# First banded attention: value matmuls moved from behind a unit's second group of scores to behind its first

## The reference

```python
def window_gqa(q, k, v, sinks):      # 16 heads of 64, 4 key heads, blocks of 128 queries
    kb, vb = bands(k), bands(v)      # each block sees the key block before, its own, and the next
    scores = jnp.einsum('bnqhgd,bnkhd->bnhgqk', qb, kb) * (ATTN_HEAD_DIM ** -0.5)
    scores = jnp.where(mask[None, :, None, None], scores, NEG)
    m = jnp.maximum(jnp.max(scores, axis=-1, keepdims=True), s)      # s: a sink logit per head
    p = jnp.exp(scores - m)
    probs = p / (jnp.sum(p, axis=-1, keepdims=True) + jnp.exp(s - m))
    out = jnp.einsum('bnhgqk,bnkhd->bnqhgd', probs.astype(v.dtype), vb)
```

## Time and profile before

| | us |
|---|---|
| median of 3 runs (3205.15 to 3207.88) | 3205.52 |
| the profiled execution | 3204.85 |
| its span | 3203.1 |
| PE busy | 3083.7 (96%) |
| DVE busy | 1696.3 (53%) |
| ACT busy | 1104.4 (34%) |
| POOL busy | 89.8 (3%) |

### The profile page before, as it was taken

How to read it: one execution, slowest core, us unless ns; L and a number is a source line. 1 busy time by engine, 2 the same in 40 slices (tenths; PEclk the granted TensorE clock), 3 DMA queues, 4 the chain that set the end, 5 groups by cost and what they waited for, 6 DMA issues and landing times. The chain is left out here.

```text
span 3203.1 us, 34628 instructions
## 1 busy us (share of the span) xinstructions
PE 3083.7 (96%) x14272; PEld 2390.1 (75%) x14272; DVE 1696.3 (53%) x2173; ACT 1104.4 (34%) x1723; POOL 89.8 (3%) x70
## 2 busy tenths in 40 slices
PE   8998999999999999999999999999999999999898
PEld 7885567788888888877777788888887686665566
DVE  7747854644444433589854533333334734566575
ACT  4215632311111111387732311111111415776452
POOL 0004510000000000000000000000000000000000
PEclk9999999999999999999999999999999999999999
DMA  4420011121222211211131111111111131000213
GB/s 148 114 94 1 1 73 38 48 79 66 79 66 73 72 48 45 86 47 47 64 114 33 47 46 47 50 49 47 46 48 52 53 119 33 20 20 14 92 56 110
DMA packets 54510, 190.96 MB, mean 60 GB/s; under 512 B 6288, under 2 KB 6672, under 8 KB 54224
## 3 DMA queue, kind: packets, MB, share of 16 engines
q1 hardware_dynamic: 54352, 188.74, 18.0%
HBM read 172.73 MB, written 14.68 MB: 59 GB/s over the span
## 5 line engine op out<-in xcount | busy, mean ns | idle before, releaser
L285 PE MATMUL PS<-H,wsp 128*128 128x512 f32 x6864 | 1615.3, 395 | 42.3 <-DVE wsp L141 16.8
L285 PEld LDWEIGHTS PS<-H,wsp 128*128 128x128 f32 x6864 | 1291.9, 189 | 349.6 <-issue 40.6
L285 PE MATMUL PS<-p,wsp 128*128 128x512 f32 (+1 forms) x3840 | 896.0, 393 | 20.8 <-DVE p L141 20.8
L285 PEld LDWEIGHTS PS<-p,wsp 128*128 128x128 f32 x3840 | 711.9, 189 | 198.7 <-ACT wsp L138 21.6
L138 ACT ACTIVATE p<-p 128x1024 f32<-128x1024 f32 (+7 forms) x426 | 360.8, 871 | 862.1 <-DVE p L144 680.5
L138 ACT ACTIVATE wsp<-raw 128x1024 fp32r<-128x1024 f32 (+1 forms) x267 | 276.9, 1040 | 694.2 <-PE PS L285 486.7
L141 DVE TENSOR_TENSOR p<-p,PS 128x1024 f32<-128x1024 f32 (+2 forms) x232 | 244.4, 1054 | 498.7 <-PE PS L285 498.7
L141 DVE TENSOR_TENSOR wsp<-raw,wsp 128x1024 fp32r<-128x1024 f32 (+1 forms) x267 | 321.7, 1207 | 156.1 <-ACT wsp L138 150.5
L141 DVE TENSOR_TENSOR p<-PS,p 128x1024 f32<-128x1024 f32 (+2 forms) x116 | 131.0, 1130 | 372.2 <-PE PS L285 347.3
L141 DVE TENSOR_TENSOR p<-p 128x1024 fp32r<-128x1024 f32 (+5 forms) x239 | 239.6, 1010 | 115.2 <-ACT p L138 112.1
L285 PE MATMUL PS<-p 128*64 128x256 f32 (+9 forms) x1432 | 279.1, 457 | 8.8 <-ACT p L138 3.1
(11 more groups left out here) (70 smaller groups left out, 1058.6 us busy)
## 6 DMA issues: line engine op xcount, KB each, us to landing
raw<-in_in_dram SPq DMA_DIRECT2D x72, 512.0 KB, 3.6
raw<-in_dn_dram SPq DMA_DIRECT2D x65, 512.0 KB, 3.5
raw<-in_up_dram SPq DMA_DIRECT2D x64, 512.0 KB, 3.5
raw<-in_out_dram SPq DMA_DIRECT2D x42, 512.0 KB, 3.5
p<-in_ada_dram SPq DMA_DIRECT2D x24, 512.0 KB, 4.5
p<-in_x_dram SPq DMA_DIRECT2D x16, 512.0 KB, 7.7
raw<-in_kv_dram SPq DMA_DIRECT2D x16, 512.0 KB, 3.6
spill_dram<-p SPq DMA_DIRECT2D x16, 512.0 KB, 3.0
```

Source lines behind the costliest of these rows:

```text
L285: return pe(lambda e: e.matmul(o, l, r, start=start, stop=stop, **kw), *a)
```

## The change

```diff
@@ attention_units, the loop over iterations u and groups j
                     for _ in range(fills[u] if fill and early else int(bool(fill) and fills[u] > 1)):
                         fill.pop(0)()
-                    if j == J - 1 and u >= 2:
+                    if j == (0 if full else J - 1) and u >= 2:
                         values(u - 2)
```

## The result

| | before | after |
|---|---|---|
| median, us | 3205.34 (3201.59 to 3207.88, 4 runs) | 3226.59 (3223.38 to 3228.7, 4 runs) |
| profiled span, us | 3203.1 | 3221.6 |
| first scores of the stage, at us | 246.26 | 243.43 |
| first matmul of the next stage, at us | 430.74 | 450.68 |
| length of the stage, us | 184.48 | 207.25 |

The ratio is 1.0068 (95% interval 1.0055 to 1.008): slower by 21 us, where 3226 was forecast. Between the two profiled executions the stage grew by 22.8 us; it began 2.8 us earlier in the one of after, and the rest behind it was 1.4 us shorter. These two differences lie in code that the change does not touch. The earlier start goes back to TensorE's clock well ahead of the stage: behind a wait of PE for DVE of 2.1 us, at the same instructions in both traces, the granted clock from 92 to 96 us was 0.73 in the execution of before and 1.00 in that of after.

What follows compares the result with a forecast made beforehand. PE was taken as the bound, with DVE and short waits close behind. Middle +18.7, end +1.6, start +1.8 and tail -1.25 sum to +20.9 us, giving 3226 us, range 3218 to 3238.

Steps and rivals of the forecast that it cites:

- The loop: Middle of the stage, one second scores to the next: a chain through softmax, copy, values and turn, 6.63 us against 5.83.
- The hand-over from copy to matmul: From the start of ACT's first copy to the value matmul that waits for it: taken as 0.64 us.
- second scores of unit 1 to unit 4: Start of the stage: three intervals, 5.75 us for the first and 5.15 for two, together 16.05: +1.8 us.
- unit 4 to unit 28: Middle of the stage: 24 intervals of 6.63 us, less 0.51 for shorter first values, 158.6 us: +18.7.
- unit 28 to unit 31: End of the stage: short groups at 5.15 us, the first interval 5.66, together 15.96: +1.6 us.
- unit 31 to the last values: Tail of the stage: a gain, 6.24 us in place of 7.49: -1.25 us.
- The chain itself: In the tail, a short group's second scores through softmax and first copy to the waiting value matmuls: 3.55 us.
- the third rival: PE falls to 1.2 GHz in part of the stage: 3242 us for one unit in four, 3291 for all; chance 0.06.
- The first: Rival: values ahead of the turn hide its waits and PE runs without a gap, -10.6 us, 3195; chance 0.04.
- The second: Rival: the new wait at the values is balanced by the turns' waits and unseen slack, 3205.5 us; chance 0.03.
- The fourth: Rival: the subtraction into H delays the second scores' reduction in every second unit, +4 us, 3230; chance 0.05.
- my 0.5: Estimated slack on DVE: subtraction done 1.5 us after the values end, next reduction due at 2.06, some 0.5 us left.

Runs made afterwards that it cites:

- the last experiment: The changed kernel in iterations 4 to 31, with the order of before in iterations 2, 3, 32 and 33: 3221.7 us, ratio 1.0057.

## Why the prediction was right

**The loop.** The step "the values want the copy, and the copy stands behind the second group's exponentials" held. The sum was 6.63 us a unit, the trace has 6.59. The largest deviation of a term is the step from the values to the turn behind them, 1.45 where the earlier trace rows had 1.52; why it is shorter was not looked into. The hand-over from copy to matmul, for which I had chosen 0.64 between 0.59 and 0.75, was 0.65.

**The terms.** Computed as in the prediction, in us, against the earlier trace rows:

| part | before | forecast | measured | 
|---|---|---|---|
| second scores of unit 1 to unit 4 | 14.21 | +1.8 | 17.42: +3.2 |
| unit 4 to unit 28 | 139.94 | +18.7 | 157.76: +17.8 |
| unit 28 to unit 31 | 14.33 | +1.6 | 15.83: +1.5 |
| unit 31 to the last values | 7.49 | -1.25 | 7.73: +0.2 |
| sum | | +20.9 | +22.8 |

These rows of the kernel after give the four bounds and the last values:

```profile
249.34 1.22 PE L285 MATMUL PS<-p 64*128 64x256 f32 x4
```
```profile
266.76 0.92 PE L285 MATMUL PS<-p 64*128 64x384 f32 x4
```
```profile
424.52 0.70 PE L285 MATMUL PS<-p 64*128 64x256 f32 x4
```
```profile
440.35 0.70 PE L285 MATMUL PS<-p 64*128 64x256 f32 x4
...
444.15 1.97 PE L285 MATMUL PS<-p 128*64 128x256 f32 x8 [2.42 <-ACT p L138]
...
448.08 1.08 PE L285 MATMUL PS<-p 128*64 128x256 f32 x8 [0.47 <-ACT p L138]
```

**Where it was off.** The tail. I expected a gain, because a turn and H left the path there. The chain itself was 0.25 us longer than forecast (444.15 - 440.35 = 3.80, forecast 3.55). PE had only one turn to do meanwhile and waited 2.42 us; behind that wait the granted clock fell (the values took 1.97 us instead of 1.08), and values to last values took 3.93 us, where 2.69 was forecast. That is the fall of the third rival at this one place, worth 1.2 us. It need not come with the wait: the last experiment's tail had a wait of 2.51 us without it.

In the start the values came in time (253.50 - 249.34 = 4.16, forecast 4.15), but they and the turn behind them ran at the lower clock, until about 256.2, which made the first interval 1.1 us longer than forecast. The last experiment shows that this happens with the old order too. The sum had PE at full speed in the terms of the start and of the tail.

The stage grew by 22.8 us in the trace, 1.9 more than forecast, and the code outside it took 4.3 us less than in the execution of before. The medians differ by 21.3, with an interval of 18 to 26 us. So that the time came within 1 us of the forecast is luck; the 18 us in the middle are not.

**The rivals.** The first (values in front of the turn hide its waits) came true in its first half: the turns' waits are gone. In the trace of the kernel before they were 6.5 us for ACT's copies and 5.0 for DVE's in the whole stage, while the new wait is 41.3, so what they gave back is far less than what the new wait costs. The second (no change) is excluded. The third (the clock falls) is excluded for the middle, where the clock was 1.00. The fourth (DVE late) was close: behind the subtraction into H the reduction still waited 0.28 us for PE, so DVE had 0.28 us to spare and not my 0.5.

```profile
352.35 0.69 DVE L141 TENSOR_TENSOR H<-PS,H 128x512 fp32r<-128x512 f32 x1 [0.96 <-ACT H L138]
...
353.33 0.96 DVE L501 TENSOR_REDUCE sm<-PS 128x2 f32<-128x768 f32 x1 [0.28 <-PE PS L285]
```

## What to carry to other kernels

Moving an instruction group earlier in a queue moves cover as well as work: ask for which chain it was the cover, and add that chain up from the instruction behind which the gap opens to the one that closes it. If that sum is larger than the work left in between, the difference is paid in every iteration. Where an engine finishes a long softmax ahead of a short copy that another engine waits for, the place of the copy in its queue decides (15 us of 21 here). And a subtraction that waits for another engine's result is better placed behind the work that doesn't (0.3 us in each unit with H here).

## What the runs showed of the hardware

- Waits of 1.25 us in each 6.59 us left the granted clock at 1.00 over 110 us, with PE 81% busy. With waits of 2.07 us in every second unit, and shorter ones in the others, it was 0.96 (290 to 380 us of the kernel with H at its old place).
- The length of the stretch at 1.2 GHz behind the first softmax is not a property of the order: 5.3 us in the kernel before (249.39 to 254.65), 12.5 us with the same order in these iterations (246.26 to 258.71, last experiment), and some 9.7 us in the changed kernel (246.56 to 256.22).
- One and the same wait can bring the lower clock or not. Behind PE's wait of 2.1 us for DVE ahead of this stage, at the same instructions, the clock from 92 to 96 us was 0.73 in the execution of before and 1.00 in that of after. It fell in three of the nine profiled executions, those of the kernels with the matmul order of before; whether that is chance is open.
- POOL's scaling of 128x384 values takes 1.47 us where DVE takes 0.42 (L529 and L148 in the same units of these traces), and became what the turn waited for as soon as the values no longer covered it.
